# Forget-gate prompt attention: ScalarE copies three of four groups of turned probabilities, VectorE the fourth

## The reference, cut to what matters

```python
def fox_attention(q, q_pos, k, v, logf):
    c = jnp.cumsum(logf.astype(F32), axis=1)
    ...
    def block_fn(qb, pos):
        ...
        s = jnp.einsum('bqgrd,blgd->bqgrl', qg, kf) + (c_q - c_k[:, None])
        p, _ = masked_softmax(s, (kpos[None, :] <= pos[:, None])[None, :, None, None, :])
        return (jnp.einsum('bqgrl,blgd->bqgrd', p, vf).reshape(B, Q, H, D),)
    (o,) = sweep_queries(block_fn, q, q_pos)
```

## Time and profile before

| | before |
|---|---|
| median of 3 runs | 3611.28 us (3607.32 to 3617.34) |
| the profiled execution, its own time | 3590.15 us |
| its span, first to last instruction | 3588.3 us |
| mean granted TensorE clock | 0.921 of full |
| TensorE busy | 3189.9 us, 89% |
| VectorE busy | 1459.8 us, 41% |
| ScalarE busy | 988.7 us, 28% |
| GpSimd busy | 596.9 us, 17% |

### The profile page before, as it was taken

One profiled execution on the slowest core, in us unless ns is written; L12 is line 12 of the kernel. 1 busy time (PEld: TensorE's weight loads), 2 busy tenths in 40 slices (PEclk: granted clock), 3 DMA queues, 4 the chain that ended last, 5 costly groups with the idle time before them and its releaser, 6 DMA issues. The chain is left out here.

```text
span 3588.3 us, 66202 instructions
## 1 busy us (share of the span) xinstructions
PE 3189.9 (89%) x22697; PEld 2105.6 (59%) x22697; DVE 1459.8 (41%) x4164; ACT 988.7 (28%) x2334; POOL 596.9 (17%) x953
## 2 busy tenths in 40 slices
PE   8999997999999898998767768899978878999968
PEld 4355446988888655565435544466645655666633
DVE  3100101444444245555345548322147664555522
ACT  1000000323323255566113321100035542344311
POOL 0000002222221000000114535100011112333200
PEclk9989998999999779998687979999989998999979
DMA  5533555444443132223468966434132208999751
GB/s 183 203 124 129 181 199 135 136 123 124 122 123 90 35 90 59 81 60 93 142 225 279 302 197 234 156 123 144 43 88 66 67 23 298 336 329 338 254 199 73
DMA packets 331488, 556.73 MB, mean 155 GB/s; under 512 B 70930, under 2 KB 213466, under 8 KB 327482
## 3 DMA queue, kind: packets, MB, share of 16 engines
q1 hardware_dynamic: 252212, 346.29, 30.4%
q0 software_dynamic: 54256, 174.12, 15.1%
q10 hardware_dynamic: 24700, 32.09, 2.6%
HBM read 490.59 MB, written 118.25 MB: 170 GB/s over the span
## 5 line engine op out<-in xcount | busy, mean ns | idle before, releaser
L344 PE MATMUL PS<-even_w,even_xT 128*128 128x512 f32 (+1 forms) x1152 | 491.7, 586 | 2.0 <-DMA even_w<-in_w_in_e 2.0
L1222 PE MATMUL PS<-cmp_xT,cmp_w 128*128 128x255 f32 (+2 forms) x2176 | 487.2, 375 | 1.1 <-DVEq L1302 1.1
L1222 PEld LDWEIGHTS PS<-cmp_xT,cmp_w 128*128 128x128 f32 x2176 | 393.7, 191 | 47.6 <-issue 1.2
L1109 ACT ACTIVATE cmp_xT<-PS 64x512 f32<-64x512 f32 x260 | 154.8, 596 | 930.4 <-PE PS L1193 928.8
L344 PEld LDWEIGHTS PS<-even_w,even_xT 128*128 128x128 f32 x1152 | 220.8, 194 | 254.7 <-issue 248.8
L1109 DVE COPY cmp_xT<-PS 64x512 f32<-64x512 f32 x260 | 179.3, 690 | 290.2 <-PE PS L1193 288.3
L344 PE MATMUL PS<-odd_w,odd_xT 128*128 128x368 f32 x896 | 289.2, 479 | 1.4 <-DVE odd_xT L293 1.4
L300 DVE COPY even_o<-PS 128x512 f32<-128x512 f32 (+3 forms) x81 | 50.3, 622 | 441.4 <-PE PS L344 427.5
L344 PEld LDWEIGHTS PS<-odd_w,odd_xT 128*128 128x128 f32 x896 | 169.0, 193 | 100.4 <-issue 5.4
L1128 POOL DMA_DIRECT2D cmp_pairs<-in_cache_nsa x256 | 151.5, 599 | 388.0 <-issue 388.0
L1852 POOL DMA_DIRECT2D s_fox_kv<-in_cache_fox x256 | 137.5, 537 | 284.0 <-issue 265.1
(11 more groups left out here) (451 smaller groups left out, 4677.5 us busy)
## 6 DMA issues: line engine op xcount, KB each, us to landing
s_fox_kv<-in_cache_fox SPq DMA_DIRECT2D x256, 256.0 KB, 7.3
s_fox_kv<-in_cache_fox POOLq DMA_DIRECT2D x256, 256.0 KB, 6.9
cmp_pairs<-in_cache_nsa SPq DMA_DIRECT2D x256, 128.0 KB, 2.9
cmp_pairs<-in_cache_nsa POOLq DMA_DIRECT2D x256, 128.0 KB, 3.0
s_sel_kv<-in_cache_nsa POOLq DMA_DIRECT2D x256, 128.0 KB, 4.5
s_sel_kv<-in_cache_nsa SPq DMA_DIRECT2D x256, 128.0 KB, 4.6
out_dil_sample<-in_cache_dil_w SPq DMA_DIRECT2D x8, 4088.0 KB
even_w<-in_w_in_e SPq DMA_DIRECT2D x8, 2048.0 KB, 8.2
```

Of the source, the lines that this page charges most:

```text
L344: last = nc.tensor.matmul(bank(c, t, 128)[:, 0:n], xT[:, k, t * 128:t * 128 + 128], w[:, c % WS, k, 0:n], start=(k == 0), stop=(k == KT - 1))
L1109: last = nc.vector.tensor_copy(dst, x) if l else nc.scalar.activation(dst, x, ACT.Copy)
L1222: last = nc.tensor.matmul(hidden_ps(x, NK)[:, g], w1[:, kv, c, :], xT[:, u % 2, kv, g, c % 8, at:at + NK], start=(c == 0), stop=(c == 15))
```

## The change

The copies of the forget-gate stage are shared out by another rule. Of four groups in a row, ScalarE copies the first three and VectorE the fourth: group g is VectorE's where g % 4 is 3. In the first call of `prompt_pairs` (no `fox` pair) the share is 2, which is the rule of before. `copied_by(e, g)` is how many of the groups below g engine e copies; TensorE's waits use it. What is turned, in what order, the two banks and the order of each engine's other work stay.

```diff
--- before.py
+++ after.py
@@ -707,6 +707,11 @@
         def t_at(g, kw, a, b):
             return PS[0:kw, 2048 + 512 * (g % 2) + a:2048 + 512 * (g % 2) + b]
         PREP, OUT = 3072, 3584
+
+
+        share = 4 if any_fox else 2
+        owner = lambda g: 1 if g % share == share - 1 else 0
+        copied_by = lambda e, g: g // share if e else g - g // share
 
         def groups(i):
 
@@ -856,7 +861,7 @@
                     kw = KW[p]
                     at = -1
                     for g, _, places in groups(i):
-                        hold(copied[g % 2], g // 2)
+                        hold(copied[owner(g - 2)], copied_by(owner(g - 2), g - 1))
                         for x, (h, j) in enumerate(places):
                             if h != at:
                                 hold(prob, 2 * i + h + 1)
@@ -867,8 +872,8 @@
                 def values(i):
                     p, n = steps[i]
                     kw = KW[p]
-                    hold(copied[0], (group_at[i + 1] + 1) // 2)
-                    hold(copied[1], group_at[i + 1] // 2)
+                    hold(copied[0], copied_by(0, group_at[i + 1]))
+                    hold(copied[1], copied_by(1, group_at[i + 1]))
                     if n == 0:
                         hold(v_in[kv_of[p] % 2], by_kv(n_v, p))
                     if n % 4 == 0:
@@ -973,7 +978,7 @@
                 def copies(i):
                     p, n = steps[i]
                     for g, x, places in groups(i):
-                        if g % 2:
+                        if owner(g) == 1:
                             dve.wait_ge(turned, g + 1)
                             n = 128 * len(places)
                             V.tensor_copy(pT[0:KW[p], i % 2, 128 * x:128 * x + n], t_at(g, KW[p], 0, n)).then_inc(copied[1], 1)
@@ -1029,7 +1034,7 @@
                 def copies(i):
                     p, n = steps[i]
                     for g, x, places in groups(i):
-                        if g % 2 == 0:
+                        if owner(g) == 0:
                             act.wait_ge(turned, g + 1)
                             n = 128 * len(places)
                             nc.scalar.activation(pT[0:KW[p], i % 2, 128 * x:128 * x + n], t_at(g, KW[p], 0, n), ACT.Copy).then_inc(copied[0], 1)
```

## The result

| | before | after |
|---|---|---|
| median, us (20 runs each) | 3610.9 | 3589.3 |
| ratio, 95% interval | | 0.9942 [0.9923, 0.9961] |
| profiled execution, us | 3590.15 | 3589.83 |
| forget-gate stage in it, us | 315.91 | 297.21 |

What follows compares the result with a forecast made beforehand. TensorE was taken to fill the forget-gate stage, losing time to waits for late VectorE copies and a lowered clock. 13.8 + 11.65 - 3.1 = 22.4 us saved, so 3611.3 - 22.4 = 3588.9, said as 3589 us; range 3583 to 3605.

Steps and rivals of the forecast that it cites:

- group 9's wait: Ahead of group 11, ScalarE copies group 9 sooner; TensorE starts 1.74 us earlier in pair 1, saving 13.8 us over the stage.
- three signs: Clock below 1.00 from group 11 to step 7, group 11 over 1.6 us after group 10's end, or turnings waiting for exp.
- the sum: Over the forget-gate stage: 13.8 us from group 9, plus 11.65 from the clock, minus 3.1 at group 14: 22.4 us saved.
- the first rival: Clock still falls in pairs 2, 4 and 6, losing 6.9 us: gain 15.5 us, 3595.8 us; chance 0.20.
- Lateness at group 14: Group 14 waits for group 12's copy behind exp of step 7: 0.46 us in pairs 1 to 6, 3.1 us in all.
- The clock: From group 11 to the turning of step 7, the clock stays up after the shorter wait: gain 11.65 us.
- The clock in all pairs: Rival: the clock falls in every pair as before, losing all 11.65 us: gain 10.7 us, 3600.6 us; chance 0.12.
- Group 5 buys nothing: At step 6's limits, VectorE arrives 0.6 us sooner but waits that much longer beside GpSimd; the 1.7 us waits stay.
- Groups 1, 13 and 17: Other moved copies: no cost counted; bounds 0.6 us a pair for group 1, 2 us in all for group 13.
- ScalarE as the pace: Rival: TensorE comes to wait for exp behind five more copies a pair, 10.2 us slower, 3621.5 us; chance 0.05.
- a gain that only moves: Rival: group 9's 1.74 us come back at group 12 or 13; about 3 us gained without clock, 3608 us; chance 0.09.

Runs made afterwards that it cites:

- e1: Kernel before, with only group 9's copies given to ScalarE: stage 299.00 us against 315.91, ratio to before 0.9949.
- e9: Changed kernel, with identity turnings keeping TensorE busy ahead of groups 9 and 11 in pairs 2, 4 and 6: stage 292.57 us against 297.21, ratio to before 0.9935.
- e2: Kernel before, with groups 1, 5, 13 and 17 given to ScalarE but group 9 left on VectorE: stage 319.86 us against 315.91, ratio 1.0015.
- e7: Changed kernel, but ScalarE copies all 20 groups of a pair and VectorE none: stage 297.25 us against 297.21, ratio to before 0.9946.
- early mask: GpSimd adds pair p+2's mask, not p+1's, ahead of its store of pair p: stage 308.69 us in before, 279.78 in after, 304.76 with group 9 alone moved.
- e12: Changed kernel, profiled and timed once more without a new edit: stage 296.59 us, ratio to before 0.9946.
- e3: Kernel before, with 14 identity turnings keeping TensorE busy ahead of its wait for group 9's bank: stage 307.54 us against 315.91, ratio 0.9985.
- e4: Kernel before, with GpSimd's mask addition issued one store earlier: stage 308.69 us against 315.91, ratio 0.9977.
- e5: Changed kernel, with GpSimd's mask addition issued one store earlier: stage 279.78 us against 297.21, median 3571.1 us, ratio to before 0.9899.

## Why the prediction was right, and which term was mis-sized

The mechanism was the one predicted in its main term, group 9's wait, and the time came out as forecast. Part of that closeness is luck: the stages of the two pairs of profiles say 18.7 and 19.3 us where the sum said 22.4 and the first rival 15.5, and the medians' 21.6 us are uncertain by 7 either way. Of the three signs that would show the forecast wrong, one was there: the clock was below 1.00 in three of the seven stretches (0.69, 0.93 and 0.72). The other two were not: group 11 never started 1.6 us after group 10's end, and TensorE waited for an exp once, 1.27 us, as before.

**Group 9's wait: right.** Waits for group 11 came to 0.34, 1.35, 1.35, 1.35, 0.50, 1.18, 1.28 and 0.73 us in pairs 0 to 7, 8.1 in all, against 23.2 before: 15.1 us. From it goes 0.9 us, as the three waits for group 7 grew. That is 14.2 us for the 13.8 of the sum, and e1 shows that it belongs to this one copy.

**Lateness at group 14: right in sum.** Pair 1 has 7.90 us from group 11 to step 7 and pairs 3 and 5 have 7.55, against 7.21: 0.69 and 0.34 where 0.46 was charged. In pair 7 the wait at group 14 grew by 0.82 us (0.34 to 1.16), where 0.3 was charged. Over the stage these waits grew by 2.8 us, for 3.1 in the sum. TensorE's idle time fell by 11.9 us where 13.8 - 3.1 = 10.7 had been worked out.

**The clock: this term was mis-sized.** "I take it that the clock stays up, and count all 11.65 us." Busy time fell by 6.8 us (8.3 between the second profiles). The step that failed took the 1.35 us left as the only wait that counts, and pair 0's 2.03 us as a length that does no harm. In pairs 2, 4 and 6 the wait of 2 us ahead of group 9 stands close in front of it. This is pair 2:

```profile
2745.37 4.67 POOL L794 TENSOR_TENSOR fox_tbd<-fox_tb,causal 128x1024 f32<-128x1024 f32 x2
...
2746.92 3.39 DVE L974 TENSOR_TENSOR fox_o<-fox_o,fox_m 128x2 f32<-128x2 f32 x2
...
2751.45 1.07 PE L869 MATMUL PS<-ident,fox_S 128*128 128x128 f32 x8 [1.97 <-DVE fox_pT L984]
...
2753.87 1.08 PE L869 MATMUL PS<-ident,fox_S 128*128 128x128 f32 x4 [1.35 <-ACT fox_pT L1040]
```

Group 9's eight turnings still take 1.07 us, group 11's four already 1.08 instead of 0.63. That is the first rival, which had been given 0.20: true in pairs 2 and 6 in both profiles of after, and in pair 4 in part in the first and not at all in the second. Against pairs 3 and 5 the windows lose 2.29 and 1.98 us, and pair 4 loses 0.08 and, at group 9, 0.85. e9 took such gaps away and the clock came back. Nor is 2 us alone a safe length: in pair 4 the clock was low already at group 9, behind 2.11 us alone.

**The clock in all pairs: wrong.** Pairs 1, 3 and 5 run at 1.00 after their 1.35 us waits. The rule of the Trainium skill ("TensorE: Matmul & The Clock Gate", section "A second HAM failure mode: psum-queue depth-cycling"), that short idle spells between groups of matmuls set the clock swinging, is not borne out by these pairs; pairs 2 and 6 show it for two longer ones in a row.

**Group 5 buys nothing: right in sum, half right in detail.** L974 took 3.39, 3.35 and 3.38 us in pairs 2, 4 and 6, as forecast (3.4), but 2.81, 2.75 and 2.74 in pairs 1, 3 and 5. There VectorE had to wait for TensorE's logits before it (0.52 us in the timeline of pair 1), so the copy it was spared made it no earlier. In pair 2 group 9 starts 6.09 us after GpSimd's mask does in before and 6.08 us after it in e1 and in after: the mask sets its time, with group 5 moved or not. TensorE only comes there sooner, and the wait is 1.97 instead of e1's 1.72 us. Groups 1, 13 and 17 cost nothing: e2 has the pairs' lengths of before, and behind the stage's start e1, without any of the four, is as long as after to 0.6 us. VectorE's 188 busy us instead of 184: the stretch is the longer one (212.1 - 27.4 = 184.7), 1.8 us are L974's, and the rest I did not trace.

**ScalarE as the pace, and a gain that only moves: wrong.** e7 rules the first out. For the second, the waits at group 14 are all that came back, 2.8 us in all, at most 0.82 in a pair.

## What to carry to other kernels

Before moving work between two engines that both have room, find the one instruction that another engine waits for, and what stands ahead of it in its in-order queue: one of five moved copies brought nearly everything. Count a wait of the engine that fills the stage at its length, and where rows show that the clock fell behind such a wait, or behind two with little work between them, add what the slower clock costs (1.5 to 2.7 us a pair here) as a bound, since the same waits did not bring it down every time. When an operation that blocks a neighbour is moved, look at what stands behind the blocked one at the new place: the same early mask was worth 17.4 us with the late copies on ScalarE, and cost 5.8 us with them on VectorE; in before, where VectorE also had group 9, it was worth 7.2 us.

## What the runs showed of the hardware that was not expected

- The granted clock fell to the 1.2 GHz level after waits of 1.97 and 1.35 us (pair 2 of after) with 1.07 us of turning between them, and not after any of the twelve single waits of 1.18 to 1.35 us in pairs 1, 3 and 5 of after, e12, e1 and e9. But the lengths of the waits do not decide it. A single wait of 2.03 us left the clock at 1.00, one of 1.85 us in e2 was followed by 0.80, and about 1.6 us behind the filling of e3 by 1.00 three times and by 0.81 twice. Of two single waits of 2.49 us in e4 one was followed by 0.81 and one by 1.00, and 1.71 and 1.35 us in pair 6 of e1 by 1.00. The windows from group 11 to the turning of step 7 are, for pairs 2 and 4 of e4 and pair 6 of e1:

```profile
2751.00:2759.83 8.83, 8.59 (x75) 6.71 (x75) 4.06 (x17) 3.63 (x10) 4.52 (x2) 0.81 0.74 199
2825.18:2832.39 7.21, 6.87 (x74) 5.25 (x75) 3.97 (x18) 3.63 (x10) 2.77 (x2) 1.00 0.92 240
2899.82:2907.33 7.51, 6.77 (x74) 5.26 (x75) 4.53 (x27) 4.56 (x11) 0.00 (x0) 1.00 0.01 2
```

- VectorE's operation on 128x2 elements, 0.17 us when undisturbed (L977 in e5), took 2.23 us beside GpSimd's mask and ended with it (2717.25 + 2.23 = 2719.48; 2714.79 + 4.67 = 2719.46). The Trainium skill ("SBUF — State Buffer", section "SBUF: two separate sides") describes the ports that both engines share as an exclusive lock held for the whole instruction; the row agrees in its length. Where it says that VectorE's side needs two inputs in SBUF or one of its faster modes, this operation has one tensor input; whether it ran in such a mode no run here shows.
